# A layer step on one core: the sums over partitions of squares as two float32r products instead of one float32 product

## What is computed

```python
def rmsnorm(x, g):
    xf = x.astype(F32)
    xf = xf * lax.rsqrt(jnp.mean(xf * xf, axis=-1, keepdims=True) + EPS)
    return xf.astype(x.dtype) * g
...
    qa = rope(rmsnorm(qa.reshape(b, t, A_HEADS, 2, A_DH), p['q_norm_g']), pos)
    ka = rope(rmsnorm(ka.reshape(b, t, A_HEADS, 2, A_DH), p['k_norm_g']), pos)
    ...
    oa = rmsnorm(oa, p['subln_g']) * (1.0 - p['lam_init'])
    ...
    ob = rmsnorm(ob, p['hgrn_norm_g']) * jax.nn.silu(ogb.astype(F32).reshape(b, t, B_HEADS, B_DV))
```

## Time and profile before

| | |
|---|---|
| median of 3 runs | 2321.14 us (2319.52 to 2322.29) |
| span of the profiled execution | 2317.6 us |
| busy: PE, DVE, ACT, POOL | 2283.8, 1433.6, 1046.8, 805.3 us |
| head stage | about 80 to 1104 us |
| TensorE's clock granted, head stage | 1.00 of full speed |
| 42 sums L985 (84 records), one record | 454 ns |
| 32 sums L1049 (64 records), one record | 592 ns |

### The profile page before, as it was taken

One profiled execution on the slowest core, in us unless ns is written; L12 is line 12 of the kernel. 1 busy time (PEld: TensorE's weight loads), 2 busy tenths in 40 slices (PEclk: granted clock), 3 DMA queues, 4 the chain that ended last, 5 costly groups with the idle time before them and its releaser, 6 DMA issues. The chain is left out here.

```text
span 2317.6 us, 46133 instructions
## 1 busy us (share of the span) xinstructions
PE 2283.8 (99%) x18425; PEld 2153.4 (93%) x18425; DVE 1433.6 (62%) x2594; ACT 1046.8 (45%) x2114; POOL 805.3 (35%) x1019
## 2 busy tenths in 40 slices
PE   7999999999999999999999999999999999999999
PEld 5898989989898989899888999999999999999999
DVE  5667676777676776765787324337546545555557
ACT  6656656556566656564333321125333333332331
POOL 1143342626252434424444124442222323222222
PEclk9999999999999999999999999999999999999999
DMA  7213121222312131211899413111111111111113
GB/s 299 92 47 103 41 87 59 73 77 57 102 54 95 49 101 49 92 46 53 326 346 347 159 61 104 46 48 51 46 46 46 46 46 46 54 43 51 46 46 99
DMA packets 75057, 213.19 MB, mean 92 GB/s; under 512 B 15579, under 2 KB 23643, under 8 KB 74843
## 3 DMA queue, kind: packets, MB, share of 16 engines
q1 hardware_dynamic: 73690, 206.05, 26.6%
q10 hardware_dynamic: 1152, 4.19, 0.4%
HBM read 175.49 MB, written 26.26 MB: 87 GB/s over the span
## 5 line engine op out<-in xcount | busy, mean ns | idle before, releaser
L170 PE MATMUL h_G<-xn_hi,h_w_hi 128*128 128x344 f32 x1368 | 457.7, 335 | 0.2 <-ACT h_d_oraw L897 0.2
L170 PE MATMUL h_G<-xn_hi,h_w_lo 128*128 128x344 f32 x1368 | 437.1, 319 | 0.0
L170 PE MATMUL h_G<-xn_lo,h_w_hi 128*128 128x344 f32 x1368 | 436.5, 319 | 0.0
L2419 POOL TENSOR_TENSOR h_w_lo<-h_w_raw,h_w_hi 128x1024 fp32r<-128x1024 f32 x87 | 215.7, 2480 | 488.8 <-DVE f_y L2620 208.7
L2341 PE MATMUL t_ps<-hn_hi,h_w_hi 128*128 128x344 f32 x1024 | 327.7, 320 | 0.9 <-issue 0.9
L2341 PE MATMUL t_ps<-hn_lo,h_w_hi 128*128 128x344 f32 x1024 | 327.1, 319 | 0.0
L2341 PE MATMUL t_ps<-hn_hi,h_w_lo 128*128 128x344 f32 x1024 | 327.0, 319 | 0.0
L1167 POOL TENSOR_TENSOR h_w_lo<-h_w_raw,h_w_hi 128x1024 fp32r<-128x1024 f32 x58 | 149.2, 2572 | 432.6 <-ACT h_w_hi L764 365.0
L170 PEld LDWEIGHTS h_G<-xn_hi,h_w_hi 128*128 128x128 f32 x1368 | 258.4, 189 | 32.5 <-issue 21.5
L170 PEld LDWEIGHTS h_G<-xn_lo,h_w_hi 128*128 128x128 f32 x1368 | 257.1, 188 | 4.4 <-issue 0.2
L170 PEld LDWEIGHTS h_G<-xn_hi,h_w_lo 128*128 128x128 f32 x1368 | 257.1, 188 | 0.0
(11 more groups left out here) (403 smaller groups left out, 5510.3 us busy)
## 6 DMA issues: line engine op xcount, KB each, us to landing
h_w_raw<-in_w_in SPq DMA_DIRECT2D x72, 512.0 KB, 3.8
h_w_raw<-in_w_ffn SPq DMA_DIRECT2D x66, 512.0 KB, 3.6
h_d_ada_w<-in_w_ada SPq DMA_DIRECT2D x32, 512.0 KB, 4.3
g_kp<-in_cache_k SPq DMA_DIRECT2D x32, 512.0 KB, 7.1
g_vp<-in_cache_v SPq DMA_DIRECT2D x32, 512.0 KB, 5.6
h_w_raw<-in_w_mix SPq DMA_DIRECT2D x24, 512.0 KB, 3.6
x<-in_xT SPq DMA_DIRECT2D x16, 516.0 KB, 7.5
n_ada_w<-in_w_ada SPq DMA_DIRECT2D x16, 512.0 KB, 13.8
```

The source lines that it names most:

```text
L170: ins = eng.matmul(out, w[:, k * P:(k + 1) * P], x[:, k, columns], start=(k == 0 and n == 0), stop=(k == n_k - 1 and n == 2))
L2419: pool.tensor_tensor(wlo[buf(n)][:, :], raw[n % 2][:, :], whi[buf(n)][:, :].bitcast(F32), ALU.subtract).then_inc(w_lo.sem, 1)
```

## The change

A sum of squares becomes two float32r products that add up in PSUM: of the squares' high part, and of the squares less this high part. The matrices `blk` and `ones128` are copied to float32r tiles once, ahead of the loop.

For queries and keys ACT makes the high part straight from PSUM (a Square that writes float32r, `sq_hi`), then the plain Square as before; POOL subtracts (`piece_low`), and PE waits for that too (`qk_lo`). For the head outputs ACT squares `oraw` and `braw` a second time into float32r tiles (`o_square`), and POOL subtracts in place behind its own squaring. The new tiles lie in memory that is free at the time. The six sums ahead of the loop (L995) stay as they are.

```diff
+            def next_piece(g, ps, u):
+
+                act.activation(sq_hi[u % 2][:, :], ps, ACT.Square)
+                qk_piece(g, ps, sq[u % 2][:, :], rg[u % 2][:, :])
+
+            def o_square(h, src, u):
+
+                s = slice((u % 2) * 512, (u % 2) * 512 + 512)
+                act.activation(squares_high(h, u), src[:, s], ACT.Square).then_inc(o_hi.sem, 1)
...
+            act.activation(blk_r[:, :], blk[:, :], ACT.Copy)
+            act.activation(ones_r, c["ones128"][:, :], ACT.Copy).then_inc(rounded.sem, 1)
...
+            def rec_squares(h):
+                act.wait_ge(o_read.sem, o_read.at(h + 1, 0))
+                o_square(h, braw, 2)
+                o_square(h, braw, 3)
+
             for h in range(H):
+                if h:
+                    rec_squares(h - 1)
...
+                    if k in SQUARES_AT:
+                        act.wait_ge(pv_read.sem, pv_read.at(h, NB))
+                        o_square(h, oraw, SQUARES_AT.index(k))
...
             def qk_sums(u):
-                pe.matmul(X[:, u, 0:TH], blk[:, :], sq[u][:, :], start=True, stop=True).then_inc(qk_summed.sem, 1)
+                pe.matmul(X[:, u, 0:TH], blk_r[:, :], sq_hi[u][:, :], start=True, stop=False)
+                pe.matmul(X[:, u, 0:TH], blk_r[:, :], sq_lo[u][:, :], start=False, stop=True).then_inc(qk_summed.sem, 1)
...
             def o_sum(h, u):
-                pe.wait_ge(o_squared.sem, o_squared.at(h, u + 1))
-                pe.matmul(X[:, sum_bank(h, u), :], ones[:, :], rstd_o[:, (u % 2) * 512:(u % 2) * 512 + 512],
-                          start=True, stop=True).then_inc(o_summed.sem, 1)
+                pe.wait_ge(o_hi.sem, o_hi.at(h, u + 1))
+                pe.wait_ge(o_lo.sem, o_lo.at(h, u + 1))
+                pe.matmul(X[:, sum_bank(h, u), :], ones_r, squares_high(h, u), start=True, stop=False)
+                pe.matmul(X[:, sum_bank(h, u), :], ones_r, o_sq_lo[:, (u % 2) * 512:(u % 2) * 512 + 512],
+                          start=False, stop=True).then_inc(o_summed.sem, 1)
...
                         pe.wait_ge(qk_squared.sem, qk_squared.at(h, k + 1))
+                        pe.wait_ge(qk_lo.sem, qk_lo.at(h, k + 1))
...
             def squares(h, src, u):
                 s = slice((u % 2) * 512, (u % 2) * 512 + 512)
-                pool.tensor_tensor(rstd_o[:, s], src[:, s], src[:, s], ALU.mult).then_inc(o_squared.sem, 1)
+                ch(pool.tensor_tensor(rstd_o[:, s], src[:, s], src[:, s], ALU.mult))
+                ch.sync()
+                pool.wait_ge(o_hi.sem, o_hi.at(h, u + 1))
+                pool.tensor_tensor(o_sq_lo[:, s], rstd_o[:, s], squares_high(h, u).bitcast(F32), ALU.subtract).then_inc(o_lo.sem, 1)
+
+            def piece_low(h, u):
+
+                if u < 6 and not no_next(h):
+                    pool.wait_ge(qk_squared.sem, qk_squared.at(h, u + 1))
+                    pool.tensor_tensor(sq_lo[u % 2][:, :], sq[u % 2][:, :], sq_hi[u % 2][:, :].bitcast(F32), ALU.subtract).then_inc(qk_lo.sem, 1)
...
                 split_next(h, FILL_PIECE)
+                piece_low(h, 0)
                 for k in range(NB):
...
                         pool.sem_inc(sample_rec.sem, 1)
+                    piece_low(h, k + 1)
                     if k in SQUARES_AT:
```

More of the change, by code:

```diff
@@ L545, in heads_stage @@
         LK = [mem(f"LK{i}", [P, LEVELS, P]) for i in range(2)]
-        LQ = [mem(f"LQ{i}", [P, LEVELS + 1, P]) for i in range(2)]
+        LQ = []
+        for i in range(2):
+            lq1_at = mem.off
+            LQ.append(mem(f"LQ{i}", [P, LEVELS + 1, P]))
         braw = mem("braw", [P, T])
@@ L564, in heads_stage, with shared @@
         AN, AR = spot("near_products", [P, FINE + 1, QUAD]), spot("near_sum", [P, QUAD])
+        def shared(name, tile, columns):
+            return nc.alloc_sbuf_tensor_at(f"h_{name}", [P, columns], F32R, offset=tile)
+        at_h_d = R3 + WIDE + ROW
+        sq_lo = [shared(f"sq_lo{i}", at_h_d + (4 + i) * TH * 4, TH) for i in range(2)]
+        sq_hi = [shared(f"sq_hi{i}", R3 + i * TH * 4, TH) for i in range(2)]
+        o_sq_hi = {"att": shared("att_sq_hi", R3 + 2 * TH * 4, T), "last_att": shared("last_att_sq_hi", at_h_d, T),
+                   "rec": shared("rec_sq_hi", lq1_at, T)}
+        o_sq_lo = shared("o_sq_lo", rstd_o_at, T)
+        ones_r, blk_r = c["ones128_r"][:, :], shared("blk_r", early["blk_at"], P)
         G, SP_, X = banks
@@ L612, in heads_stage @@
         st_stored = S("state_stored", 1, step=16, init=1)
-        o_squared, o_summed, o_rstd, o_normed = S("o_squared", 4), S("o_summed", 4), S("o_rstd", 4), S("o_normed", 4, init=1)
+        o_hi, o_lo, o_summed, o_rstd, o_normed = S("o_sq_hi", 4), S("o_sq_lo", 4), S("o_summed", 4), S("o_rstd", 4), S("o_normed", 4, init=1)
+        qk_lo, rounded = S("qk_sq_lo", 6), S("blk_ones_rounded", 0)
         a_stored, b_stored = S("att_stored", 2, step=16), S("rec_stored", 2, step=16)
@@ L643, in no_next, with squares_high @@
             return h == H - 1
+        def squares_high(h, u):
+            tile = o_sq_hi["rec" if u >= 2 else "last_att" if no_next(h) else "att"]
+            return tile[:, (u % 2) * 512:(u % 2) * 512 + 512]
         def weight(h, t):
@@ L968, in _ @@
                 ch.reset()
+            rec_squares(H - 1)
             piece(H, 0)
@@ L1131, in _ @@
                         pe.wait_ge(qk_squared.sem, qk_squared.at(h, k + 1))
+                        pe.wait_ge(qk_lo.sem, qk_lo.at(h, k + 1))
+                        if h == 0 and k == 0:
+                            pe.wait_ge(rounded.sem, 1)
                         if k >= 2:
```

8 lines of the change are left out of this document (6 added, 2 removed).

## The result

| | before | changed kernel |
|---|---|---|
| median of the runs | 2320.52 us (2319.52 to 2322.29) | 2349.88 us (2344.77 to 2353.93) |
| ratio | 1 | 1.0124, 95% interval 1.0110 to 1.0138 |
| span of the profiled execution | 2317.6 us | 2351.9 us |
| start of the stage behind the head stage | 1104.37 us | 1129.92 us |

The change costs 29.4 us; +19.0 was forecast. The profiled execution of the changed kernel is its slowest run; of its 34.3 us, 25.6 arise in the head stage and 8.8 behind it.

What follows compares the result with a forecast made beforehand. PE was taken to bound the kernel. Waits of 6.0 us per repeating head, x7 = +42.0, plus 1.2 at the stage's end, less 24.2 of gain, gave +19.0 us: 2340, range 2326 to 2352.

Steps and rivals of the forecast that it cites:

- What a sum costs PE: Two float32r products for one float32 save 0.265 us per 344-column sum, 0.40 per 512-column sum; gain on PE 24 us.
- rival D: The products save less than they should, the wide one 0.25 instead of 0.40: +5 us, 2345; within the main forecast's 0.60.
- The costs on POOL and ACT: Added subtractions on POOL take 0.92 us (344 columns) and 1.28 (512); ACT's extra Squares 0.34 and some 0.6.
- Chunk 0: First turn of the recurrent loop: POOL subtracts behind the weight split, so PE waits 2.33 us for sum 0.
- Chunk 1: Second turn of the recurrent loop: PE waits 0.83 us for POOL's subtraction ahead of sum 1.
- Chunks 2 to 5: Later loop turns: PE waits for sums 0.7 us in chunk 3, 0.4 in 5, 0.15 in 2 and 4; together 1.25.
- the ring: DVE's longer rounds make PE wait 0.6, 0.4 and 0.6 us ahead of products of chunks 4, 5, 6; 1.6 per head.
- Ends of the stage: Last rec sum of the head stage costs +1.2 us; later heads' starts 0, at most 0.3 x 7.
- A: Rival: only direct waits count, 4.56 us per head, DVE loses no time: +8.9, 2330; chance 0.16, short end (2322) 0.06.
- B: Rival: POOL's and ACT's new work hides, gain comes whole: 2297; decides at 3.4 us of waits per head; chance 0.05.
- C: Rival: each subtraction and squaring holds a DVE product in full, 7.4 us per head: +31, 2352; chance 0.13.

Runs made afterwards that it cites:

- e6: Kernel before, with q/k sums as one float32r product of the rounded squares alone, no second Square, subtraction or wait: 2320.37 us, ratio 0.9995.
- e7: The change with POOL's first subtraction ahead of the weight split and the later ones ahead of the five small copies: 2334.03 us, ratio 1.0055.
- e10: Kernel before, without DVE's product with the sine: 2317.02 us, ratio 0.9986.
- e2: The change for the q/k sums only; sums over head outputs stay one float32 product as in the kernel before: 2350.58 us, ratio 1.0126.
- e8: Edits of e7, plus POOL's squaring and subtraction of both attention output halves moved from chunks 2 and 4 to chunk 6: 2331.46 us, ratio 1.0038.
- e12: The change without DVE's product with the sine: 2341.65 us, ratio 1.0092.
- e4: The change with all added work and waits, but each sum one float32 product of the high part alone: 2368.15 us, ratio 1.0202.

## Why the prediction was right or wrong

The sign, the mechanism and most terms held; the size was 10 us short.

**What a sum costs PE: right.** Two sums over a head's outputs in the changed kernel, which answer to the earlier trace rows:

```profile
203.17 0.39 PE L1098 MATMUL h_X<-h_att_sq_hi,keep_ones_r 128*128 128x512 f32 x1
203.40 0.39 PE L1099 MATMUL h_X<-h_o_sq_lo,keep_ones_r 128*128 128x512 f32 x1
203.63 0.39 PE L1098 MATMUL h_X<-h_att_sq_hi,keep_ones_r 128*128 128x512 f32 x1
```

A product of 512 columns holds PE 0.23, the value taken, and two sums save 0.79 in two places of a head (0.80 forecast). Of the 344 columns e6's 0.40 fits the 0.58 and 0.157. The sign named for it, sums that hold PE for 0.31, does not show: the rows have 0.40 from the first product to the piece. But where the sum is not waited for (e7, chunk 0) its first product starts 0.08 behind the transposition in place of 0.16, and from the transposition to the piece PE takes 0.48 instead of 0.75, 0.26 less (0.265 forecast). That makes rival D wrong. What was wrong is that these savings count in full: e6 shows that of a saving at the q/k sums alone 0.4 of 2.5 us a head is left, because DVE is as late. In the change itself it still counted, since there PE's waits made it the later one in most chunks.

**The costs on POOL and ACT: right.** The subtraction of 344 columns takes 0.92 (forecast 0.92), that of 512 a median of 1.29 for the recurrence output and 1.37 for the attention output (1.28), the rounded Square 0.34 to the next instruction.

**Chunk 0: right.** Wait 2.33, forecast 2.33, for the reason given. POOL and PE of head 0, as the earlier trace rows:

```profile
155.45 2.36 POOL L1220 TENSOR_TENSOR h_w_lo<-h_w_raw,h_w_hi 128x1024 fp32r<-128x1024 f32 x1 [0.27 <-POOL h_b_level_diff L1252]
157.76 0.91 POOL L1267 TENSOR_TENSOR h_sq_lo<-h_d_sq,h_sq_hi 128x344 fp32r<-128x344 f32 x1
```

```profile
158.77 0.40 PE L1032 MATMUL h_X<-h_sq_hi,h_blk_r 128*128 128x344 f32 x1 [2.09 <-issue]
```

**Chunk 1: right.** 0.52 + 0.265 = 0.79, forecast 0.83. (By the starts PE stands 1.0 us at sum 1. Of the 0.2 us that DVE costs in this step before, by e10, the prediction knew nothing; the wait covers it.)

**Chunks 2 to 5: the step that failed is chunk 4.** With the saving of 0.265 added back, the steps are 0.18, 0.85, 1.36 and 1.18, 3.6 in all; the prediction had 0.08, 1.3, 0.47 and 1.0, 2.85. That the sums are no farther apart is in part luck: chunk 3 was sized 0.45 too high and chunk 4 0.89 too low. The prediction gave chunk 4 no more than some hundredths for the sum and 0.4 for the ring. There PE sits idle for 0.69 ahead of sum 4, 0.93 by the starts. POOL, head 1, from its turn k = 2 of the loop (PE is in chunk 3 by then) to the subtraction for sum 4:

```profile
307.36 1.03 POOL L1267 TENSOR_TENSOR h_sq_lo<-h_d_sq,h_sq_hi 128x344 fp32r<-128x344 f32 x1 [0.29 <-ACT h_d_sq L792]
308.36 1.31 POOL L1258 TENSOR_TENSOR h_d_rstd_o<-h_d_oraw 128x512 f32<-128x512 f32 x1
309.74 1.29 POOL L1261 TENSOR_TENSOR h_o_sq_lo<-h_d_rstd_o,h_att_sq_hi 128x512 fp32r<-128x512 f32 x1
...
313.88 0.93 POOL L1299 TENSOR_TENSOR h_d_rg<-h_d_rg,h_cos 128x344 f32<-128x344 f32 x1 [0.24 <-POOL h_b_level_diff L1252]
314.77 0.91 POOL L1267 TENSOR_TENSOR h_sq_lo<-h_d_sq,h_sq_hi 128x344 fp32r<-128x344 f32 x1
```

Sum 4's subtraction ends at 315.68 and PE starts at 315.78. It is late because a narrow subtraction, a squaring and a wide subtraction stand in a row in turn 2, ahead of the differences and the cosine product of the turn behind; from 307.36 on POOL waits 0.24 us at most. Without the wide subtraction (e2) or with it in chunk 6 (e8) step 4 is -0.08 or -0.07. A part comes from VectorE: L1258 takes 1.31 above, held in its turn by L1335 (307.65 to 308.76), and in e12, which has one VectorE product less,

```profile
308.33 1.04 POOL L1258 TENSOR_TENSOR h_d_rstd_o<-h_d_oraw 128x512 f32<-128x512 f32 x1
```

There the idle time at sum 4 is 0.43 instead of 0.69. The prediction counted the wide subtraction only as a load on DVE, not as one on POOL's own next turn.

**The ring: right in kind, smaller, and elsewhere.** Forecast were waits of 0.6, 0.4 and 0.6 ahead of the products of chunks 4, 5 and 6; they are 0, 0.36 and 0.82, 1.2 together (1.3 by the starts), and e12 gives 1.1, of which 0.26 is the shorter wait at sum 4. The sign named for it was wrong: L1269 (L1333 in the changed kernel) was to last 1.3 in chunks 0, 1 and 3. All heads, before and changed (ns: least, median, most):

```profile
L1269 DVE TENSOR_TENSOR h_d_rt<-h_d_rt,h_sin x42: 516/518/1341, 162.0 to 953.1; 128x344 f32<-128x344 f32 x42
```

```profile
L1333 DVE TENSOR_TENSOR h_d_rt<-h_d_rt,h_sin x42: 516/518/1266, 162.7 to 981.2; 128x344 f32<-128x344 f32 x42
L1335 DVE TENSOR_TENSOR h_d_rg<-h_d_rg,h_d_rt x42: 516/812/1249, 163.2 to 981.7; 128x344 f32<-128x344 f32 x42
```

In head 1 it lasts 0.52 in chunks 0 to 2 and 5. In chunks 1 and 2 POOL waits 0.4 and 0.3 us for ACT's squares behind the cosine product, and L1333 has started by then; L1335 behind it is held instead, 1.12 and 1.11. In chunk 3 it is L1333 (1.20), in chunk 4 both (1.25 and 1.24).

Of the 84 instances of L1333 and L1335 in the changed kernel 35 are held, and each of them ends 0.37 us behind a GpSimd instruction's end. The Trainium skill's rule of the exclusive pair, "SBUF — State Buffer", "Who interferes with whom", was thus borne out in every held row. What failed was the forecast of the order: who starts first decides who waits, and POOL's 0.3 us of waiting let another product start first.

**Ends of the stage: right.** The last sums start 1.0 us late by the starts, +1.2 forecast; the later heads' starts lose nothing (step 7 is -0.80, the plain saving).

**Rivals.** A (2330) fell: the waits of its kind alone are 5.4 us a head by the starts, where it had 4.56, and the 1.1 us of e12 come on top. B fell: sums 0, 1, 3 and 4 are waited for by 0.8 to 2.3 us each, and by e6 even without these waits most of the saving at the q/k sums would have been lost. C (31 us) came close in size and is wrong in kind: not every subtraction holds a product that matters. The period of a head is 130.1 to 130.3 us (131.74 in head 3, with its stretch at half clock), where the prediction had 129.4 and named 130.5 as the point from which the ring was sized too low: it was not the ring that was.

**The sum.** Forecast in the head stage +19.0; measured 25.6 in the profiled execution. The 6.6 between them are 0.7 x 7 = 4.9 of a head's steps (the sums of chunks 2 to 5 1.0 a head too light, the ring 0.3 too heavy), 1.6 from one stretch at half clock in head 3 (550.8 us), and 0.1. The medians differ by 29.4, 3.8 more than the stage. Two slips of arithmetic are in the prediction: the gains 11.1 and 12.8 make 23.9, not 24.2, and rival B's turning point of 3.4 us of waits a head leaves out the 1.2 at the stage's end; with both put right it is 3.2. Neither matters beside the 6.6.

**What stays open.** Behind the head stage the changed kernel's profiled execution loses another 8.8 us, mainly in the stage of the gates and the single tokens, where the code is unchanged. PE's longest waits there, before and changed:

```profile
PE g_Y L1740 <- DVE g_s_tok L1852: 6.0, 4, 3.3
```

```profile
PE g_Y L1804 <- DVE g_s_tok L1916: 9.4, 5, 5.2
```

and the granted clock is 0.96 there, against 0.98. Behind the head stage the stretches at half clock add up to 17.1 us in the changed kernel, 6.8 before, and 3.4 to 10.2 in the experiments; 10.2 us more of them cost at most 5.1, an estimate from half the rate, so they can be more than half of the 8.8 or a consequence of the waits. In the twelve kernels of the experiments the part behind the head stage differs from the kernel before by -0.9 to +3.0 us, with the same code, and e2, e4 and e12 among them have most of the change's work, so it does not follow that work. The runs of the change also scatter over 9 us, those of e7 over 1.2. What decides it was not found; transfers keep the DMA engines 86% busy in this stage, and where they fall against DVE's work is a candidate that no run here tests.

## What to carry over

Where two engines are late together, a saving on one is worth little (here 0.4 of 2.5 us) until the other has one too: test it by leaving the work out on each and on both. A new operation on a third engine costs through three ways, and each has to be walked: who waits for its result, which of the shared-port engine's instructions it stands beside, and what it pushes back in its own queue one turn later. The last was the one missed here.
